# First products inside the norm stages, and four changes to waits, in a two-block transformer kernel

## The reference, cut to what matters

```python
h = rms_norm(x, g_pre_ffn1[l]) * (1 + sc1) + sh1
x = x + 0.5 * gt1 * rms_norm(swiglu(h, w_gate1[l], w_up1[l], w_down1[l]), g_post_ffn1[l])
u = rms_norm(x, g_pre_mix[l]) * (1 + sc2) + sh2
y = hybrid_mixer(u, ...)           # proj = u @ w_in ... z = sigmoid(g_a) * (o_a @ w_up_a) + sigmoid(g_b) * (o_b @ w_up_b); return z @ w_o
x = x + gt2 * rms_norm(y, g_post_mix[l])
h = rms_norm(x, g_pre_ffn2[l]) * (1 + sc3) + sh3
x = x + 0.5 * gt3 * rms_norm(swiglu(h, w_gate2[l], w_up2[l], w_down2[l]), g_post_ffn2[l])

def swiglu(h, w_gate, w_up, w_down):           # 1024 -> 2816 -> 1024
    return (jax.nn.silu(h @ w_gate) * (h @ w_up)) @ w_down

# second block
h = rms_norm_2(x, g_norm1[l]) * (1.0 + sc1) + sh1
proj = h @ w_in[l]
x = x + gt1 * mixed                            # latent attention and retention, joined, @ w_out
h2 = rms_norm_2(x, g_norm2[l]) * (1.0 + sc2) + sh2
x = x + gt2 * peer(h2, w_query[l], sub_keys[l], expert_u[l], expert_v[l])

def peer(h, w_query, sub_keys, expert_u, expert_v):
    q = (xt @ w_query).reshape(T, 8, 2, 128)             # 16 groups of 128 query columns
    s = einsum('thpd,pkd->thpk', q, sub_keys)            # 128 keys for each half
    # the best 16 of each half, the best 16 pairs of each head, softmax g over them
    a = gelu(einsum('thkd,td->thk', expert_u[ib], xb))
    return einsum('thk,thkd->td', g * a, expert_v[ib])
```

## Time and profile before

| | |
|---|---|
| Median of three runs | 3187.83 us |
| The profiled execution | 3187.51 us |
| its span | 3185.7 us |
| mean granted TensorE clock | 0.947 of full |
| TensorE busy | 2881.2 us, 90% |
| VectorE busy | 2034.4 us, 64% |
| ScalarE busy | 1074.8 us, 34% |
| GpSimd busy | 819.8 us, 26% |
| DMA | 536.72 MB, 168 GB/s on average |

### The profile page before, as it was taken

The page is one execution under the profiler, slowest core; times in us unless marked ns, Lnnn a source line. Parts: engine busy times, 40 slices in busy tenths (PEclk is TensorE's granted clock), DMA queues, the critical chain, the costliest instruction groups (busy, mean ns, idle before and its releaser), DMA issues. The chain is left out here.

```text
span 3185.7 us, 37699 instructions
## 1 busy us (share of the span) xinstructions
PE 2881.2 (90%) x14118; PEld 2437.5 (77%) x14118; DVE 2034.4 (64%) x3525; ACT 1074.8 (34%) x1574; POOL 819.8 (26%) x536
## 2 busy tenths in 40 slices
PE   4899996988879789998898779999989999999998
PEld 4788874875567667887675568998989999898776
DVE  6673745547742243232645429989769989898887
ACT  1221214233342232122334333555633333333333
POOL 0000000000001000000000023766767777776220
PEclk9999997988789889999898889999999999999999
DMA  7774821200023223332210113566688888888995
GB/s 271 239 249 146 256 100 66 90 25 16 14 55 92 79 80 92 93 96 71 67 42 17 54 69 114 176 194 203 195 326 331 328 325 322 313 322 315 353 348 196
DMA packets 298413, 536.72 MB, mean 168 GB/s; under 512 B 12584, under 2 KB 193164, under 8 KB 280460
## 3 DMA queue, kind: packets, MB, share of 16 engines
q1 hardware_dynamic: 211696, 375.07, 34.4%
q0 software_dynamic: 36864, 134.23, 11.5%
q10 hardware_dynamic: 49692, 25.28, 2.9%
HBM read 495.73 MB, written 38.80 MB: 168 GB/s over the span
## 5 line engine op out<-in xcount | busy, mean ns | idle before, releaser
L173 PE MATMUL ps<-query_h_hi,expert_u_hi 128*128 128x384 f32 (+1 forms) x1152 | 399.5, 347 | 5.4 <-ACT expert_u_hi L2333 5.4
L173 PE MATMUL ps<-query_h_lo,expert_u_hi 128*128 128x384 f32 (+1 forms) x1152 | 395.6, 343 | 0.0
L2071 POOL TENSOR_TENSOR expert_u_lo<-feat,expert_u_hi 128x1024 fp32r<-128x1024 f32 x144 | 353.0, 2452 | 144.9 <-ACT expert_u_hi L2333 143.5
L173 PE MATMUL ps<-expert_v_hi,expert_w_hi 128*128 128x512 f32 x768 | 304.1, 396 | 15.0 <-DVE expert_w_lo L2239 12.4
L2244 DVE TENSOR_TENSOR expert_v_lo<-peer_s,expert_v_hi 128x1024 fp32r<-128x1024 f32 x128 | 214.3, 1674 | 137.3 <-ACT expert_v_hi L2341 133.7
L173 PE MATMUL ps<-expert_v_hi,expert_w_lo 128*128 128x512 f32 x768 | 301.9, 393 | 0.0
L173 PE MATMUL ps<-expert_v_lo,expert_w_hi 128*128 128x512 f32 x768 | 301.8, 393 | 0.0
L173 PE MATMUL ps<-ffn_h_hi,ffn_w_hi 128*128 128x512 f32 x704 | 278.0, 395 | 18.5 <-PEq L560 17.5
L173 PE MATMUL ps<-ffn_h_lo,ffn_w_hi 128*128 128x512 f32 x704 | 275.5, 391 | 0.0
L173 PE MATMUL ps<-ffn_h_hi,ffn_w_lo 128*128 128x512 f32 x704 | 275.4, 391 | 0.0
L221 DVE TENSOR_TENSOR ffn_w_lo<-ffn_w_raw,ffn_w_hi 128x2048 fp32r<-128x2048 f32 x66 | 151.1, 2290 | 165.1 <-ACT ffn_w_hi L217 165.1
(11 more groups left out here) (448 smaller groups left out, 6294.1 us busy)
## 6 DMA issues: line engine op xcount, KB each, us to landing
feat<-in_expert_u_blocks SPq DMA_DIRECT2D x64, 1024.0 KB
peer_s<-in_expert_v_blocks SPq DMA_DIRECT2D x64, 1024.0 KB
gate_rows<-expert_gates SPq DMA_DIRECT2D x31, 768.0 KB
ffn_w_raw<-in_w_gate SPq DMA_DIRECT2D x44, 512.0 KB, 3.9
ffn_w_raw<-in_w_up SPq DMA_DIRECT2D x44, 512.0 KB, 5.1
ffn_w_raw<-in_w_down SPq DMA_DIRECT2D x22, 1024.0 KB, 4.8
gate_rows<-in_w_mod SPq DMA_DIRECT2D x18, 1024.0 KB, 5.2
in_w_raw<-in_w_in SPq DMA_DIRECT2D x16, 1024.0 KB, 5.1
```

What stands on the lines that cost most here:

```text
L173: return nc.tensor.matmul(out, lhsT, rhs, start=start, stop=stop, skip_group_check=True)
L2071: nc.gpsimd.tensor_tensor(u_lo[:, n % 2, :, :], u_raw[:, n // 2 % 2, n % 2, :, :], u_hi[:, n % 2, :, :], ALU.subtract).then_inc(u_lo_done, 1)
```

## The change

1. `stage_norm_turn` gets `lead`: after the transposes TensorE does the products of the first gate block (FFN: 24 products) or of the whole first slot (projections: 48) in this stage, one column k after the other, as soon as the high and low part of the column are there (new semaphore `lo_done`). The later stages leave these products out.
2. The expert norm stage gets `queries`: SP loads the first pair of query weights into `peer_hots` (not yet used), ScalarE rounds them before it moves the columns, GpSimd subtracts. In `stage_peer` the numbering of `u_lo_done` and `u_hi_done` is less by 2 (ROUNDED), the first load falls away, and the turning of the sub keys goes behind the first query group.
3. Down stage: for its first slot the banks go 7, 0, 1, ... 6, and the single wait becomes one for each thing that a bank needs.
4. Output: the first slot of w_o is multiplied at the end of `stage_gated_up` (`first_slot_products`); the last z is summed and subtracted on VectorE.
5. Experts: the first two pairs of v are loaded before the last pair of u, behind a wait for all gates, and the first v and w are rounded before the last two gelus.

```diff
+            @block.gpsimd
+            def _(pool):
+                for n in range(2):
+                    pool.wait_ge(queries_hi, n + 1)
+                    nc.gpsimd.tensor_tensor(u_lo[:, n, :, :], raw[:, n, :, :], u_hi[:, n, :, :], ALU.subtract)
...
+            if queries:
+                act.wait_ge(queries_in, 16)
+                for n in range(2):
+                    nc.scalar.activation(u_hi[:, n, :, :], raw[:, n, :, :], ACT.Copy).then_inc(queries_hi, 1)
             for k in range(0, DC, 2):
                 scale, shift = factors(k + 1)
                 act.wait_ge(turned, k + 2)
...
-                nc.vector.tensor_tensor(h_lo[:, k, :], b.feat[:, k, :], h_hi[:, k, :], ALU.subtract)
+                nc.vector.tensor_tensor(h_lo[:, k, :], b.feat[:, k, :], h_hi[:, k, :], ALU.subtract).then_inc(lo_done, 1)
...
+            if lead:
+                ws, chunks, tiles = lead
+                pe.wait_ge(ws.lo_done, 1)
+                for k in range(chunks):
+                    pe.wait_ge(hi_done, k + 1)
+                    pe.wait_ge(lo_done, k + 1)
+                    for bank in range(TT if tiles else 1):
+                        if k == 0:
+                            pe.wait_ge(moved_act if bank % 2 else moved_dve, bank // 2 + 1)
+                        if tiles:
+                            w = tiles[0].shape[-1]
+                            ins = split_products(nc, b.ps[:, bank, 0:w], tiles[1](k, bank), ws.parts(0, k * w, w), k == 0, False)
+                        else:
+                            ins = split_products(nc, b.ps[:, bank, :], ws.parts(0, k * P, P), (h_hi[:, k, :], h_lo[:, k, :]),
+                                                 k == 0, k == DC - 1)
+                if tiles:
+                    ins.then_inc(ws.used, 1)
...
-                        for m in range(2):
+                        for m in range(1 if first and j == 0 else 0, 2):
...
-                    pe.wait_ge(gu_lo_done, c0 + n)
                     for q in range(n // 2):
                         m = base + n + q
                         pe.wait_ge(ws.lo_done, m + 1)
-                        for bank in range(8):
+                        banks = (7, 0, 1, 2, 3, 4, 5, 6) if q == 0 else range(8)
+                        if q == 1:
+                            pe.wait_ge(gu_lo_done, c0 + n)
+                        for bank in banks:
                             i, half = bank // 2, bank % 2
+                            if q == 0 and bank == 0:
+                                pe.wait_ge(gu_done, c0 + n - 1)
+                            if q == 0 and bank == 2:
+                                pe.wait_ge(gu_done, c0 + n)
+                            if q == 0 and bank == 4:
+                                pe.wait_ge(gu_lo_done, c0 + n - 1)
+                            if q == 0 and bank == 5:
+                                pe.wait_ge(gu_lo_done, c0 + n)
...
+def first_slot_products(nc, b, ws, jobs):
+
+    w = jobs[0][0].shape[-1]
+    for i in range(TT):
+        for k in range(DC // 2):
+            ins = split_products(nc, b.ps[:, i, 0:w], jobs[0][1](k, i), ws.parts(0, k * w, w), k == 0, False)
+    return ins
...
-                for m in range(n_slots):
+                for m in range(multiplied_slots, n_slots):
...
+                pe.wait_ge(ws.lo_done, 2 * DC + 1)
+                pe.wait_ge(read, 2 * (DC - 1))
+                pe.wait_ge(z_done, DC // 2)
+                first_slot_products(nc, b, ws, next_jobs).then_inc(ws.used, 1)
...
+                dve.wait_ge(read, 2 * DC)
+                z_m = part[:, (DC - 1) % 2, 0, :]
+                dve.wait_ge(z_sum, DC - 1)
+                nc.vector.tensor_tensor(z_m, z_m, part[:, (DC - 1) % 2, 1, :], ALU.add).then_inc(z_sum, 1)
+                dve.wait_ge(z_hi_done, DC)
+                nc.vector.tensor_tensor(z[1][:, DC - 1, :], z_m, z[0][:, DC - 1, :], ALU.subtract).then_inc(z_done, 1)
                 job_rest(ws, dve, next_jobs, 1)
...
-                    if a + 4 < AHEAD + 4:
-                        load_u(a + 4)
-                sp.wait_ge(routed, whole_at[1])
-                load_v(0)
-                sp.wait_ge(gate_up, BATCHES)
-                load_v(2)
+                    if a == AHEAD - LAST:
+                        sp.wait_ge(routed, whole_at[1])
+                        load_v(0)
+                        sp.wait_ge(gate_up, BATCHES)
+                        load_v(2)
+                    load_u(a + 4)
...
                 for a in range(AHEAD - LAST, AHEAD):
+                    if a == AHEAD - 2:
+                        v_round(0)
+                        w_round(0)
                     gelu(a)
                     u_round(G + a + 2)
...
-        stage_norm_turn(nc, b, "nt5", 4, 12, *h, keep_tokens=b.tok[:, TT - 1, :])
-        stage_peer(nc, b, d, h, out)
+        more_hots = own.enter_context(nc.sbuf_tensor("peer_hots", [P, 2, D], F32))
+        u_hi, u_lo = (own.enter_context(nc.sbuf_tensor(f"expert_u_{part}", [P, 2, DC, P], F32R)) for part in ("hi", "lo"))
+        first = (d["w_query_blocks"][0], more_hots[:, :, :].rearrange("p o (k c) -> p o k c", k=DC), u_hi, u_lo)
+        stage_norm_turn(nc, b, "nt5", 4, 12, *h, keep_tokens=b.tok[:, TT - 1, :], queries=first)
+        stage_peer(nc, b, d, h, out, more_hots, u_hi, u_lo)
```

73 lines of the change are left out of this document (39 added, 34 removed).

## The result

The changed kernel takes 3142.28 us (median of four executions, 3135.32 to 3154.64) beside 3193.72 us of the kernel before (four executions, 3182.13 to 3201.18): ratio 0.985, 95% interval 0.9815 to 0.9885. It is faster by 1.5%, 51 us. The prediction was 3129 us with a range of 3114 to 3158. The profiled execution took 3135.32 us, its span is 3133.4 us, 52.3 less than that of before. TensorE's mean granted clock rose from 0.947 to 0.955.

A forecast was written before the change was run, and what follows sets the result against it. TensorE, busy 90% of the span, was taken as the bound, so earlier starts carry to the end. Terms 22 + 13.9 + 8.7 + 3.5 + 10.6 = 58.7 us off 3187.51 gave 3129 us, range 3114 to 3158.

The forecast's parts named there:

- Leads: Four norm stages of FFNs and projections: first products start inside the stage, 5.5 us each, 22 us; bounds 4.5 to 6.6 each.
- What was late next: After the leads: projections' slot 2 ready 2 us before it is needed; in the FFNs, 16 us of products cover it.
- Down stages: Four down stages: most of each 2.8 us wait for the hidden tile's last low part goes; 13.9 us, bounds 10 and 14.5.
- The term for the clock: Down stages: 1.2 GHz stretches of 3.4 us behind two of the four waits go, 1.6 us each.
- Output projection: First slot starts 7.6 us sooner, pays 0.5, regains 1.6 from the clock: 8.7 us; bounds 6 and 9.
- start of the expert stage: First query weights prepared in the norm stage: 6.7 us saved less 3.0 gives 3.5 us; bounds 0.5 and 6.
- From the dots to the sums: Expert stage, v rows loaded early: 12.3 us won, 1.7 lost to a new w low part wait; 10.6, bounds 6 and 12.5.
- Untouched stages: Stages that the change does not touch: 0 us predicted.
- rival 1: New waits in projections' slot 2 and the expert stage take back much of the gain: 34 us, 3153 us; chance 0.17.
- rival 2: Norm stages: clock stays at 1.2 GHz as products come column by column, leads give about nothing; 3151 us; chance 0.08.
- rival 3: Expert stage: VectorE is the true bound, both earlier starts give nothing and steps may lengthen; 3158 us; chance 0.06.
- rival 4: Expert sums: earlier v loads shift the queue, 72 steps with dots grow; at 0.9 us each 3194 us; chance 0.04.

The follow-up runs named there:

- experiment 5: Changed kernel with the down stages' bank order and waits put back as before; 3155.14 us, ratio 0.9871 to the kernel before.
- experiment 4: Changed kernel with w's low part for the second step of the sums taken ahead of the own row's dot product on VectorE; 3147.11 us.
- experiment 8: Changed kernel with the edit of experiment 4, and GpSimd's low part of the next u row moved between the first gathers; 3142.22 us.
- experiment 9: Kernel of experiment 8 with the 2 MB residual loaded 44 steps before the sums' end, not at their start; 3138.13 us.
- experiment 3: Changed kernel with unused filler products keeping TensorE busy in the five norm stages; 3123.56 us, ratio 0.9789 to the kernel before.
- experiment 12: Changed kernel with experiments 3 and 8, and the residual loaded late in two parts, 44 and six steps before the end; 3120.74 us.
- experiment 10: Kernel of experiment 3 with eight filler products also in the sparse attention behind its first scores; 3144.25 us, ratio 0.9843 to the kernel before.

## Why the prediction was right

The forecast was a gain of 58.7 us; the traces give 52.3 and the medians 51. All parts of the change did what was said. Losses that were not in the sum are 2.2 us in the first FFN and 3.7 in the sums, the leads gave 1.9 us less, and the 1.4 us that stages without any change gave are luck. The range's low end took 5 us for the difference between runs of one kernel, where the three runs it was made from lie 19 us apart.

**Leads (22, measured 20.1).** The mechanism is as put: 24 products in 8.2 us at the end of the norm stage, TensorE never starved, the debit at the stage's end 0.3. The forecast took a slow stretch of 5 us; it is 3.9 to 5.4. The first FFN gave only 4.3 because the stretch that it replaced had been the shortest seen, 3.55 us. It lies just under the lower bound of 4.5. What was late next came out otherwise than forecast: in the projections slot 2 was in time with 1.7 us to spare, and in the first FFN, where 16 us of products were to cover it, it was 0.7 us late. There VectorE has 6 us of the modulation's work in front of the low part, for rows that landed only at 100.33 us, so the low part ended at 108.5; the forecast had left that out.

**Down stages (13.9, measured 11.9; 15 when undone).** The waits for the hidden tile's low part went entirely; at the first start 0.56 us for the down weights came in their place, where 0.2 was taken. The table puts the two losses of the first FFN, 0.7 and 1.5 us, to this part; without them it gave 14.1. The slow stretch at 296 us stands at this place in ten of the twelve experiments' traces and not in the one trace of the kernel before; why is open. The term for the clock, two times 1.6, is an average over something that changes from run to run: two slow starts before, three in experiment 5.

**Output projection (8.7, measured 8.3)** and **start of the expert stage (3.5, measured 3.8)** came as worked out, the second with its debit: 2.2 us for VectorE beside GpSimd, where 2.5 were taken.

**From the dots to the sums (10.6, measured 6.8).** This is the step that was mis-sized. The forecast had 12.3 us won and one new wait of 1.7 for the second w low part, and nothing behind it. By the same products in both traces the changed kernel wins 12.5 us until the end of the first sums, and then gives back 5.6 (6.9 in all; the table's 6.8 is read from another instruction): 0.3 in the dots, 2.5 at a wait of 2.32, 1.6 in a slow stretch behind it (the granted clock over 4 us is 0.57), and 1.1 at a second wait of 0.82. So the wait itself was 0.8 too small, and the clock behind it and the second wait, 2.7 together, stood at nothing. The working had VectorE reach the second v low part half a us ahead of GpSimd's pair and be held in it. In the trace that low part is done before the pair (it ends at 2278.77, the pair begins at 2279.61); VectorE then stands 2.15 us for the gathered row of its own product, a wait that the working did not have, and so the product begins inside the pair and takes 4.51 us in place of 1.2. The two errors nearly cancel in the first wait: w's low part was forecast 10.1 us behind the last dots and came after 11.0.

```profile
2277.54 1.23 DVE L2308 TENSOR_TENSOR expert_v_lo<-peer_s,expert_v_hi 128x1024 fp32r<-128x1024 f32 x1 [4.66 <-ACT expert_v_hi L2404]
...
2286.00:2290.00 4.00, 3.94 (x10) 3.13 (x11) 1.23 (x2) 0.15 (x1) 1.67 (x2) 0.57 1.00 418
```

Experiments 4, 8 and 9 show that neither order cures it: the rows come late because the sums begin with all their loads at once. Without the residual's 2 MB they land after 7.6 us in place of 12.5.

**Untouched stages (0, measured +1.4 net).** Single stages moved by 4.3 and −2.6 us with not an instruction changed.

**The rivals.** New waits took back 5.6 us, clock and all, in the sums, 0.7 in the first FFN and nothing in the projections (rival 1, with 24 us, was far too much). Column by column the clock rose in the leads and stayed up in experiment 3 with waits of 0.17 and 0.29 us between groups of products, so rival 2 falls; the rule of the Trainium skill beside it ("TensorE: Matmul & The Clock Gate", "A second HAM failure mode: psum-queue depth-cycling") is not borne out by these stages. VectorE is not the bound (rival 3), and the loads do not lengthen the steps (rival 4): 400 us inside the sums hold 397.6 us of products, 5.03 of them per us, before as after. VectorE's late low parts do hold single steps, as above.

```profile
2350.00:2750.00 400.00, 397.58 (x2012) 361.74 (x2011) 360.52 (x383) 134.55 (x192) 302.93 (x182) 1.00 0.89 324
```

## What to carry to other kernels

When work is moved up against another engine's pair of long instructions, price each instruction that will lie inside that pair, not the pair, and ask whether its data will be there before the pair begins. After an idle stretch ask which clock the first products will run at: an earlier start wins the idle time, and only a TensorE that was kept busy wins the slow stretch as well (11 us by the trace here, against 20 for the four earlier starts). And when a stage begins with many loads at once, look for the one that is not wanted yet: moving 2 MB away from the sums' start won 4.4 us there, which two reorderings of instructions had not; loaded later in one piece they cost as much there (experiment 9), in two parts they did not (experiment 12).

## What was not expected of the hardware

TensorE can be busy 49.58 of 50 us and be granted 1.2 GHz throughout (experiment 10, sparse attention), while in the norm stages 2.4 GHz came 3.9 to 5.4 us after the first product. The rows of this case do not say what sets the two apart. And a gap of the same length at the same place costs a slow stretch in one trace and none in another: 2.77 us at the first down stage (experiment 5 and before), 1.3 us ahead of the first FFN's second part (the changed kernel and before).

The sparse attention alone makes two executions of the same instructions differ by 13 us. With TensorE kept busy in the norm stages six executions lay within 4.6 us and five of the last kernel within 6.0, against 19 for the four of the changed kernel. Whether that is the earlier clock or the shifted moment at which the sparse attention begins was not tried.
